# A block kernel whose first down-product slices take their low parts from GpSimd

## The reference

```python
h2 = rms_norm(x, norm_mlp[layer])
u = jax.nn.relu(h2 @ w_mlp_up[layer])      # (512, 8192)
x = x + (u * u) @ w_mlp_down[layer]        # (8192 -> 2048)
```

## Time and profile before

| | |
|---|---|
| median of 3 runs | 2639.74 us (2639.61 to 2642.86) |
| profiled execution, its own time | 2639.95 us |
| its span, first to last instruction | 2638.2 us |
| mean granted clock of TensorE | 0.999 of full speed |
| busy: PE, DVE, ACT, POOL | 99%, 75%, 47%, under 4% (86.1 us) |

### The profile page before, as it was taken

How to read it: one execution, slowest core, us unless ns; L and a number is a source line. 1 busy time by engine, 2 the same in 40 slices (tenths; PEclk the granted TensorE clock), 3 DMA queues, 4 the chain that set the end, 5 groups by cost and what they waited for, 6 DMA issues and landing times.

```text
span 2638.2 us, 43303 instructions
## 1 busy us (share of the span) xinstructions
PE 2619.7 (99%) x16484; PEld 2367.9 (90%) x16484; DVE 1977.0 (75%) x2848; ACT 1246.5 (47%) x1648; POOL 86.1 (3%) x134
## 2 busy tenths in 40 slices
PE   9999999999999999999999999999999999999999
PEld 8999998888888888888889999999998999999998
DVE  4648885566666644444599899898899999999997
ACT  5534443555555543223454445445455444444444
POOL 1000000000000000000000000000000000000000
PEclk9999999999999999999999999999999999999999
DMA  7444434333333344544435554544466666566554
GB/s 256 116 133 129 127 120 132 96 84 88 92 85 88 89 124 135 148 136 144 152 118 170 180 178 167 176 164 145 149 214 209 189 186 177 171 186 198 177 187 132
DMA packets 370071, 392.25 MB, mean 149 GB/s; under 512 B 22024, under 2 KB 341512, under 8 KB 369424
## 3 DMA queue, kind: packets, MB, share of 16 engines
q1 hardware_dynamic: 341680, 312.00, 38.6%
q0 software_dynamic: 8784, 30.96, 4.9%
q10 hardware_dynamic: 19472, 47.46, 4.8%
HBM read 323.20 MB, written 67.13 MB: 148 GB/s over the span
## 4 chain that ended last, share of the span: by engine, by line
PE 83%; DVE 12%; ACT 2%; DMA 2%; issue 1%; SPq 0%; ACTq 0%; DVEq 0%; POOL 0%; POOLq 0%
PE shared L2170 7%; DVE lo L1593 5%; PE shared L2174 4%; PE job L2025 3%; PE job L2028 3%; PE job L2027 3%; PE job L2195 2%; PE scores L2195 2%; PE job L2197 2%; PE job L2196 2%; PE scores L2196 2%; PE scores L2197 2%; PE job L2273 2%; PE job L2275 2%; PE job L2274 2%; PE stats L2196 2%
## 5 line engine op out<-in xcount | busy, mean ns | idle before, releaser
L990 ACT ACTIVATE hi<-pair 128x1792 fp32r<-128x1792 f32 x268 | 456.6, 1704 | 654.4 <-PE turned L2197 217.2
L1593 DVE TENSOR_TENSOR lo<-pair,hi 128x1792 fp32r<-128x1792 f32 x268 | 541.6, 2021 | 74.8 <-ACT hi L990 74.2
L1309 DVE TENSOR_TENSOR w_lo<-raw,w_hi 128x512 fp32r<-128x512 f32 x284 | 195.3, 689 | 194.1 <-ACT w_hi L800 150.9
L2170 PE MATMUL shared<-h,hi 128*128 128x512 f32 x960 | 261.4, 393 | 0.9 <-DVE lo L1593 0.9
L800 ACT ACTIVATE w_hi<-raw 128x512 fp32r<-128x512 f32 x160 | 101.0, 632 | 251.8 <-PE job L2028 133.1
L2170 PEld LDWEIGHTS shared<-h,hi 128*128 128x128 f32 x960 | 176.3, 188 | 37.8 <-DVE lo L1593 1.3
L1583 DVE TENSOR_TENSOR pair<-pair 128x1024 f32<-128x1024 f32 x126 | 153.3, 1217 | 2.2 <-DMA pair<-in_w_mlp_down 1.9
L2174 PE MATMUL shared<-h,lo 128*128 128x256 f32 x960 | 154.0, 282 | 0.0
L2195 PE MATMUL job<-h,hi 128*128 128x256 f32 x528 | 149.4, 283 | 0.2 <-DVE lo L1593 0.2
L2197 PE MATMUL job<-h,lo 128*128 128x256 f32 x528 | 149.4, 283 | 0.0
L2196 PE MATMUL job<-h,hi 128*128 128x256 f32 x528 | 149.3, 283 | 0.0
(11 more groups left out here) (537 smaller groups left out, 7371.1 us busy)
## 6 DMA issues: line engine op xcount, KB each, us to landing
pair<-in_w_mlp_up SPq DMA_DIRECT2D x256, 256.0 KB, 2.8
pair<-in_w_mlp_down SPq DMA_DIRECT2D x248, 256.0 KB, 3.3
h<-u_rows SPq DMA_DIRECT2D x39, 896.0 KB, 7.2
raw<-in_w_in SPq DMA_DIRECT2D x256, 128.0 KB, 2.5
u_rows<-u_blocks ACTq DMA_DIRECT2D x32, 896.0 KB, 3.6
pair<-in_w_gate SPq DMA_DIRECT2D x72, 256.0 KB, 2.9
raw<-in_w_out SPq DMA_DIRECT2D x64, 256.0 KB, 3.3
sum_rows<-blocks POOLq DMA_DIRECT2D x21, 512.0 KB, 7.9
```

Of the source, the lines that this page charges most:

```text
L990: nc.scalar.activation(pair_hi[j % 2], pairs[j][:, :, 1:8], ACT.Copy).then_inc(pair_hi_ready, 1)
L1309: nc.vector.tensor_tensor(lo, raw[:, slot, part:part + KU], hi.bitcast(F32), ALU.subtract).then_inc(split_ready, 1)
L1593: nc.vector.tensor_tensor(pair_lo[j % 2], pairs[j][:, :, 1:8], pair_hi[j % 2].bitcast(F32), ALU.subtract).then_inc(pair_lo_ready, 1)
L2170: nc.tensor.matmul(into[:, :].rearrange("p (l s) -> p l s", l=2), high[:, k, w], right(2 * j + k, a), start=(j == 0 and k == 0), stop=Fals ...
```

## The change

Four of the first ten slices (2, 4, 6 and 8) get their low part on GpSimd, with the same subtraction and on the same tiles. They are counted by a semaphore of their own, `slice_split`, and TensorE now waits for both counts. ScalarE rounds slices 4, 6 and 8 one step earlier, ahead of the weight pair of the unit at which it rounded them behind. GpSimd's four subtractions stand between its last copy of the sums and its first `store_part`. The semaphore `tri_ready` is merged into `consts_ready`, with the same waits as before.

```diff
@@ the list of semaphores
-         (params_loaded, bforget_loaded, consts_ready, tri_ready,
+         (params_loaded, bforget_loaded, consts_ready,
...
+        POOL_SLICES = (2, 4, 6, 8)
...
+        def split_by(engines, e):
+
+            return sum((i in POOL_SLICES) == engines for i in range(e + 1))
@@ gpsimd
-            pool.memset(tri, 1.0).then_inc(tri_ready, 1)
-            pool.wait_ge(tri_ready, 1)
+            pool.memset(tri, 1.0).then_inc(consts_ready, 1)
+            pool.wait_ge(consts_ready, 10)
...
+            for e in POOL_SLICES:
+                hi, lo = slots[e % 8]
+                pool.wait_ge(slice_hi, e + 1)
+                pool.tensor_tensor(lo, lo.bitcast(F32), hi.bitcast(F32), ALU.subtract).then_inc(slice_split, 1)
 
             for g in range(CLOSING):
                 store_part(g)
@@ scalar
                 n = down_unit(g, j)
+                if n in (UPS + 2, UPS + 4, UPS + 6):
+                    round_slice(n - UPS + 2)
                 round_pair(n, place(g, j), n - 1)
...
-                if g < 2:
+                if n == UPS or g < 2 and n % 2 == 1:
                     round_slice(n - UPS + 2)
@@ vector
-                if n < UPS + 7:
+                if n < UPS + 7 and n - UPS + 2 not in POOL_SLICES:
                     split_slice(n - UPS + 2)
@@ tensor
-                pe.wait_ge(slice_ready, g + 2 * j + 2)
+                pe.wait_ge(slice_ready, split_by(False, g + 2 * j + 1))
+                at_least(pe, slice_split, split_by(True, g + 2 * j + 1))
```

More of the change, by code:

```diff
@@ L327, in build @@
             sem, ("hi_ready split_ready unit_used").split())
-        (params_loaded, bforget_loaded, consts_ready, tri_ready,
+        (params_loaded, bforget_loaded, consts_ready,
          dist_ready, table_loaded, gains_ready, lam_sums, lam_exps, lam_step) = map(
-            sem, ("params_loaded bforget_loaded consts_ready tri_ready "
+            sem, ("params_loaded bforget_loaded consts_ready "
                   "dist_ready table_loaded gains_ready lam_sums lam_exps lam_step").split())
@@ L370, in build @@
                   "c_third c_fourth c_ready u_rectified u_squared copied folded shared_done").split())
-        u_stepped, u_summed = sem("u_stepped"), sem("u_summed")
+        u_stepped, u_summed, slice_split = sem("u_stepped"), sem("u_summed"), sem("slice_split")
         sum_loaded = [sem(f"sum_loaded{i}") for i in range(2)]
@@ L714, in _ @@
             pool.wait_ge(g_stored, 32 * GATE_PAIRS)
-            pool.memset(tri, 1.0).then_inc(tri_ready, 1)
-            pool.wait_ge(tri_ready, 1)
+            pool.memset(tri, 1.0).then_inc(consts_ready, 1)
+            pool.wait_ge(consts_ready, 10)
             pool.affine_select(out=tri, in_=tri, compare_op=ALU.is_ge, fill=0.0,
-                               base=0, pattern=[[1, S]], channel_multiplier=-1).then_inc(tri_ready, 1)
+                               base=0, pattern=[[1, S]], channel_multiplier=-1).then_inc(consts_ready, 1)
             pool.wait_ge(f_row_ready, 1)
@@ L2247, in forget_step @@
                     pe.wait_ge(f_stepped, 3)
-                    pe.wait_ge(tri_ready, 2)
+                    pe.wait_ge(consts_ready, 11)
                     for b in range(TB):
```

## The result

The changed kernel takes 2648.49 us, the median of 8 runs (2647.62 to 2649.98), against 2639.98 for the kernel before on the same chip (8 runs). The ratio is 1.0033, with a 95% interval of 1.0024 to 1.0042: 8.5 us slower. Forecast were 2647.2 us and a loss of 7.5. The profiled execution took 2648.41 us, its span 2646.6.

What follows compares the result with a forecast made beforehand. TensorE was taken as the bound, losing 6.8 us from D0 to D9 waiting for VectorE's queue. Between 8.9 and 6.2 us later, 7.5 was taken: 2647.2 us against 2639.74; range 2636.5 to 2650.0, the forecast's own 2645 to 2650.

Steps and rivals of the forecast that it cites:

- exclusion for whole instructions: GpSimd and VectorE operations with two SBUF inputs block each other for whole instructions; 2645.9 to 2648.7 us, chance 0.55.
- variant (a): Between D1 and D9, GpSimd gets in at VectorE's next instruction boundary; D9 at 2037.3, 8.9 us later.
- Variant (b): Between D1 and D9, GpSimd gets in only where VectorE has nothing to do; D9 at 2034.7, 6.2 us later.
- short sum: On VectorE, four GpSimd subtractions block 16.7 us and four subtractions leaving save 7.8: +8.9 us, before overlaps come off.
- No disturbance: Rival: GpSimd's subtractions run hidden and VectorE's queue shortens; 2.5 us gained, 2637.2 us; chance 0.27.
- only GpSimd suffers: Rival: VectorE keeps its port, GpSimd's subtractions are stretched; at 12 us each, 2645.9 us; chance 0.08.
- Partial: Rival: both engines slowed somewhat, or half the blocking falls into pauses; 2638 to 2644 us, say 2641; chance 0.10.

Runs made afterwards that it cites:

- slices 2 and 4: Kernel before with GpSimd making only the low parts of slices 2 and 4, roundings in the old order: 2644.40 us, ratio 1.0016.
- added reads: Kernel before plus, at four moments, two useless GpSimd subtractions of 128x896 reading two inputs from a scratch tile: 2649.92 us, ratio 1.0037.
- added writes: Kernel before plus, at four moments, four useless GpSimd fills of 128x1024 that only write: 2639.78 us, ratio 1.0001.
- the kernel with one input: Kernel before plus, at four moments, four useless GpSimd operations of 128x1024 reading one SBUF input: 2650.96 us, ratio 1.0041.
- slice 9 later: Kernel before with VectorE splitting slice 9 two units later and summing D12 and D13 one unit later, no GpSimd subtraction: 2641.89 us, ratio 1.0006.
- slices 2 and 9: Kernel before with slice 9's split and the sums of D12 and D13 later on VectorE, and slice 2 on GpSimd: 2640.47 us, ratio 1.0003.
- four pieces: Full change with each GpSimd subtraction of 128x1792 cut into four of 128x448: 2648.57 us, ratio 1.0033 against the kernel before.

## Why the prediction was right

**The mechanism.** The forecast was exclusion for whole instructions. What came is its variant (a), in which GpSimd gets in at VectorE's next boundary. It held unit by unit within 1 us: D1 1982.75 (forecast 1983.0), D2 1992.04 (1992.5), D4 2007.82 (2008.3), D6 2020.03 (2020.9), D9 2036.98 (2037.3). Only D3 came later by more than that, at 1999.36 (1997.6), by the clock of TensorE (below). Three rows of `pair<-pair` of 4.4 to 4.6 us are there, and D2 is the first late unit. Variant (b), in which GpSimd gets only VectorE's gaps, shows nowhere; twice GpSimd got in between two dependent sums 0.1 us apart, and at 1982.50 between a low part and a sum, where VectorE's queue has no gap at all (the low part's row ends at 1982.60, the sum's starts at 1982.52).

**The sizes.** GpSimd's subtraction was estimated at 4.2 us and takes 4.05 where nothing holds it up. The loss was put at the middle of (a) and (b), 7.5; it is (a)'s, 8.9 from D1 to D9, of which 0.4 us came back ahead of D1 (1982.75 for 1983.18, although the up product's last unit began 0.64 later). By (a) alone the forecast would have been 2639.74 + 8.9 = 2648.6; the 1.3 us between forecast and median are the choice of the middle. Summed on VectorE: blocked (4.58 - 0.69) + (4.57 - 0.69) + (4.37 - 0.69) = 11.45; new waits for ScalarE 1.76 + 1.35 = 3.1; less three subtractions at 1.94, 5.8; that is 8.7 of the 8.9. The prediction's short sum also gives 8.9, but from other terms: 16.7 blocked by four subtractions less 7.8 saved, without the waits. Three blocked rows cost 11.45, slice 2 cost next to nothing, and the waits for ScalarE put 3.1 back. That this short sum comes out right is luck; the schedule of variant (a) is not, since it holds unit by unit.

The schedule has room for the first of these waits: its D4 at 2008.3 needs D3's low part to end near 1997.6, later than VectorE's own work would make it. But the text names such pauses only as places where GpSimd's work comes off, and not as what becomes of the saving. The subtraction of slice 4 stood between D3's sums and its low part and hid ScalarE's rounding of that pair; taking it away leaves VectorE waiting 1.76. The second wait, 1.35 ahead of D7's low part, has another cause. ScalarE rounded D7's pair late because it waited for TensorE to finish D5 and so free the buffer:

```profile
2019.51 1.70 ACT L1001 ACTIVATE hi<-pair 128x1792 fp32r<-128x1792 f32 x1 [1.74 <-PE stats L2210]
```

One reading needs a correction that changes no number: the earlier trace rows show six waits of TensorE in three groups, not three waits; the 4.8 us are right.

**What the prediction did not see.** It reckoned with TensorE's full clock throughout. Behind the pause of 4.02 us at D2 the changed kernel shows this:

```profile
core 0: us, PE busy (x) PEld busy (x) DVE busy (x) ACT busy (x) POOL busy (x), PEclk, DMA share, GB/s
...
1992.00:1994.00 2.00, 1.96 (x9) 1.99 (x10) 1.35 (x3) 0.55 (x1) 0.00 (x0) 0.50 0.52 134
1994.00:1996.00 2.00, 2.00 (x11) 2.00 (x10) 0.82 (x1) 2.00 (x2) 0.00 (x0) 0.50 0.97 222
...
1998.00:2002.00 4.00, 4.00 (x36) 4.00 (x35) 3.90 (x2) 0.33 (x1) 3.59 (x1) 1.00 0.41 142
```

Before, the same stretch had 1.00:

```profile
1992.00:1994.00 2.00, 1.88 (x17) 1.70 (x15) 2.00 (x2) 1.27 (x1) 0.00 (x0) 1.00 0.85 314
```

By start times D2 lasted 7.32 us for 5.04, 2.3 longer, and D4, behind its 3.27, lasted 6.39, 1.35 longer. Neither moved D9 by more than 0.1, as far as the rows tell. D3 would have ended near 2002.4, and with the delay near 2004.4, and D4's low part was done only at 2007.6. D4's delay made D5 end late, and so made the wait of 1.35 above. But `combine` behind D7 has to wait for D6, which began with its own low part and ended at 2025.14, and for ScalarE's copy (2025.40 to 2025.79); it began at 2025.91, so by an estimate from these rows VectorE would have lost all but 0.1 of that time there instead. In the kernel with slices 2 and 4 the same fall does cost. The prediction had no term for the clock, and the total came out right only because other work was later each time: that is luck.

**The rivals.** *No disturbance* falls by the rows of 4.4 to 4.6 us, and *only GpSimd suffers* with it, since GpSimd took 4.05 to 4.77 there, stretched by no more than the rest of a VectorE instruction; but where both queues are full both suffer (in the added reads two of GpSimd's subtractions took 5.43, for 1.69 each beside `combine`). *Partial* falls as well: a blocked row loses all that is left of GpSimd's instruction but 0.1 to 0.2 us, and the others lose nothing. That nothing but GpSimd's reads is behind it is shown by the added reads, which lose 9.9 us with VectorE's own work untouched, and by the added writes, which lose none.

**What stays open.** The operation of VectorE at 22.92 that kept its 0.69 beside GpSimd's line 706 is not explained; no run repeated that pair of operations. It may have waited its turn in line 706's 2.33 us, which is long beside the 0.83 of line 707, but no run shows it. Nor is it settled why VectorE loses a little less than GpSimd's instruction lasts, 3.89 us to one of 4.05 and 1.48 to one of 1.69.

## What to carry to other kernels

Before work moves from VectorE to GpSimd, look at what VectorE runs in the same microseconds: if it has both inputs in SBUF and GpSimd reads SBUF, the price is GpSimd's duration (here 4.05 us) and not nothing, against VectorE's own 1.94 us saved. Ask too whether the time saved on the full engine is time at all, or becomes a wait for the next engine, as the 1.76 us for ScalarE did. And where a wait is taken from one unit on an engine that is full, look for the next unit that waits before counting it as a gain.

## What the runs showed of the hardware

The exclusion works both ways and by turns: four GpSimd operations of one input took 5.18 us among VectorE's short sums and 8.91 among its subtractions of 128x1792. One input in SBUF on GpSimd's side is enough (0.84 us for each operation of 128x1024, 2.86 instead of 2.02); four writes of 128x1024 in 3.99 us cost VectorE nothing. VectorE's operations in `combine`, each with an input in PSUM, kept their 0.69 and 0.41 while GpSimd read.

TensorE's granted clock fell to 0.50, that is 1.2 GHz, for some 3 to 7 us at or shortly behind pauses of 3.27 to 4.02 us, and behind most of 1.84 to 2.82 us (1.84 and 2.04 in the added reads, 2.12 to 2.82 in the kernel with one input, 2.17 in slice 9 later), though it had been busy at 2.4 GHz up to each of them. One of 2.18 us (slices 2 and 9), one of 1.87 (four pieces) and all of at most 1.72 in these stretches left it at 1.00; what tells 2.17 from 2.18 no run here shows. Units of 5.04 us that met a fall took 6.35 to 7.82, 1.3 to 2.8 more. That a long pause so costs more than itself was the surprise here, and whether it shows depends on which engine is late next.
